# A two-layer transformer block with its follow-on block: weight splits reordered at the MLP entries, high halves first in narrow units

## The reference, cut to what matters

```python
h = x
for layer in range(2):
    hn = rms_norm(h, attn_norm[layer])
    ...                                        # attention
    h = h + merge_heads(mix) @ w_o[layer]
    h = h + squared_relu_mlp(rms_norm(h, mlp_norm[layer]), w_up[layer], w_down[layer])
x = rms_norm(h, final_norm)
mod = silu(c) @ w_ada + b_ada                  # 1024 x 9216
x = x + 0.5 * g1 * swiglu(modulate(rmsnorm(x), sh1, sc1), w_gate, w_up, w_down)
x = x + g2 * hybrid_mixer(modulate(rmsnorm(x), sh2, sc2), ...)
x = x + 0.5 * g3 * swiglu(modulate(rmsnorm(x), sh3, sc3), w_gate, w_up, w_down)
```

## Time and profile before

| what | value |
|---|---|
| median of 3 runs | 1197.65 us (1197.55, 1197.65, 1202.66) |
| the profiled execution: its own time | 1197.43 us |
| its span, first to last instruction | 1195.8 us |
| mean granted TensorE clock | 0.998 |
| DVE busy | 863.9 us (72%) |
| ACT busy | 652.5 us (55%) |
| POOL busy | 73.1 us (6%) |
| HBM traffic | 197 GB/s over the span |
| chain that ended last | PE 83%, DVE 8%, ACT 4%, issue 3%, DMA 1% |

### The profile page before, as it was taken

How to read it: one execution, slowest core, us unless ns; L and a number is a source line. 1 busy time by engine, 2 the same in 40 slices (tenths; PEclk the granted TensorE clock), 3 DMA queues, 4 the chain that set the end, 5 groups by cost and what they waited for, 6 DMA issues and landing times.

```text
span 1195.8 us, 17774 instructions
## 1 busy us (share of the span) xinstructions
PE 1165.1 (97%) x6763; PEld 1012.5 (85%) x6763; DVE 863.9 (72%) x1243; ACT 652.5 (55%) x883; POOL 73.1 (6%) x112
## 2 busy tenths in 40 slices
PE   8999999999999999999999999999999999999997
PEld 7898888888888888888888888888988888888886
DVE  6687799888767778988476765567986866655655
ACT  5556546555545555556565444547746755545453
POOL 9200011110000001110000000000000000000000
PEclk9999999999999999999999999999999999999999
DMA  7733699997463269997635565544661153655560
GB/s 253 229 109 124 228 333 351 316 316 251 150 192 130 71 214 352 338 320 252 212 106 190 198 207 179 195 146 145 195 209 39 32 197 122 211 179 195 168 216 36
DMA packets 143238, 236.33 MB, mean 198 GB/s; under 512 B 6357, under 2 KB 106950, under 8 KB 143174
## 3 DMA queue, kind: packets, MB, share of 16 engines
q1 hardware_dynamic: 130402, 196.73, 49.1%
q0 software_dynamic: 10400, 37.77, 8.7%
q10 hardware_dynamic: 2372, 0.96, 0.3%
HBM read 234.37 MB, written 1.05 MB: 197 GB/s over the span
## 4 chain that ended last, share of the span: by engine, by line
PE 83%; DVE 8%; ACT 4%; issue 3%; DMA 1%; POOL 0%; DVEq 0%; POOLq 0%; ACTq 0%
PE ps L2308 17%; PE ps L2062 9%; PE ps L2064 9%; PE ps L2066 9%; PE ps L2311 9%; DVE wlo L1120 3%; PE ps L1952 3%; PE ps L1954 3%; PE ps L1953 3%; PE ps L1999 2%; PE ps L2000 2%; PE ps L2001 2%; ACT whi L626 2%; PE ps L2151 1%; PE ps L2153 1%
## 5 line engine op out<-in xcount | busy, mean ns | idle before, releaser
L1120 DVE TENSOR_TENSOR wlo<-raw,whi 128x2048 fp32r<-128x2048 f32 (+2 forms) x185 | 414.9, 2258 | 134.4 <-ACT whi L626 133.9
L626 ACT ACTIVATE whi<-raw 128x2048 fp32r<-128x2048 f32 (+2 forms) x185 | 348.2, 1888 | 140.0 <-PE ps L2066 59.1
L2308 PE MATMUL ps<-a,whi 128*128 128x512 f32 x1024 | 255.7, 392 | 1.4 <-DVE wlo L1120 1.4
L2308 PEld LDWEIGHTS ps<-a,whi 128*128 128x128 f32 x1024 | 186.9, 189 | 37.0 <-issue 1.8
L2311 PEld LDWEIGHTS ps<-a,wlo 128*128 128x128 f32 x1024 | 139.8, 191 | 9.9
L2311 PE MATMUL ps<-a,wlo 128*128 128x256 f32 x1024 | 142.8, 283 | 0.0
L2062 PE MATMUL ps<-whi,hh 128*128 128x512 f32 x376 | 117.0, 393 | 3.5 <-DVE wlo L1120 3.5
L2064 PE MATMUL ps<-wlo,hh 128*128 128x512 f32 x376 | 116.3, 390 | 0.0
L2066 PE MATMUL ps<-whi,hl 128*128 128x512 f32 x376 | 116.1, 390 | 0.0
L1592 DVE SCALAR_TENSOR_TENSOR stage<-stage,cact 128x1024 f32<-128x1024 f32 x63 | 80.7, 1281 | 4.9 <-DMA stage<-in_w_ada_dram 3.6
L2064 PEld LDWEIGHTS ps<-wlo,hh 128*128 128x128 f32 x376 | 70.6, 188 | 15.2
(11 more groups left out here) (436 smaller groups left out, 1965.7 us busy)
## 6 DMA issues: line engine op xcount, KB each, us to landing
stage<-in_w_ada_dram POOLq DMA_DIRECT2D x72, 512.0 KB, 5.5
raw<-in_w_up_dram SPq DMA_DIRECT2D x32, 1024.0 KB, 6.7
raw<-in_w_down_dram SPq DMA_DIRECT2D x32, 1024.0 KB, 7.3
raw<-in_ffn_w_gate_dram SPq DMA_DIRECT2D x22, 1024.0 KB, 5.4
raw<-in_ffn_w_up_dram SPq DMA_DIRECT2D x22, 1024.0 KB, 5.4
raw<-in_ffn_w_down_dram SPq DMA_DIRECT2D x22, 1024.0 KB, 5.1
raw<-in_moba_w_qkv_dram SPq DMA_DIRECT2D x11, 1024.0 KB, 6.6
raw<-in_w_in_dram SPq DMA_DIRECT2D x10, 1024.0 KB, 5.2
```

What stands on the lines that cost most here:

```text
L626: A.activation(whi[:, s, 0:size], raw[:, s, 0:size], ACT.Copy).then_inc(w_hi, 1)
L1120: V.tensor_tensor(wlo[:, s, 0:size], raw[:, s, 0:size], whi[:, s, 0:size].bitcast(F32), ALU.subtract).then_inc(w_lo, 1)
L2308: T.matmul(bank(b + m), wh[:, c, m * P:(m + 1) * P], a2[:, c].rearrange("p k n -> p (k n)"), start=(c == 0), stop=False)
```

## The change

Six edits:

1. `a_unit` on PE: the loop is turned. For all eight tiles c and both column halves m it does the two matmuls with high weights first, waiting only for `w_hi`; then it waits for `w_lo` and does the 16 matmuls with low weights. In the very first unit this is done for c = 0 to 3 with `first_hi` and `first_lo`, then for c = 4 to 7.
2. `first_body` of both MLPs on DVE: the split of the first down unit n0+2 is done in two halves, the first with a semaphore of its own (`down_lo`); PE's first `d_unit` waits for that before k = 0 and for `w_lo` before k = 1.
3. `body(1)` of both MLPs on DVE is written out, and in it the addition (or fold) that stood between `hl` and the two splits stands between the two splits.
4. First chunk of both FFNs, on ACT and DVE: the split of unit n0+3 (the second up unit) moves ahead of the chunk; that of n0+4 stays behind it.
5. In the mixer on DVE the copy L1828 moves ahead of the split of unit U_Z+2.
6. The semaphore `down_lo` is added.

```diff
@@ -252,6 +252,7 @@
         in_ready = sem("in_ready")
         up_hi = sem("up_hi")
         up_lo = sem("up_lo")
+        down_lo = sem("down_lo")
         dstep = sem("dstep")
         astep = sem("astep")
         pstep = sem("pstep")
@@ -900,9 +901,11 @@
                         n_at = lambda q: n + q + 3 * FFN_BODY * i if isinstance(i, int) else (n + q, i)
                         split(n_at(0), slot(n))
                         if isinstance(i, int) and i == 0 and j == 0:
+                            split(n_at(1), slot(n + 1))
                             chunk(c0, n0 + 2, 4, True, 0)
-                        else:
-                            gated_chunk(i * FFN_BODY + (c0 + j), i * FFN_BODY + (k0 + j), i * (3 * FFN_BODY) + (n0 + 3 * j), j)
+                            split(n_at(2), slot(n + 2))
+                            continue
+                        gated_chunk(i * FFN_BODY + (c0 + j), i * FFN_BODY + (k0 + j), i * (3 * FFN_BODY) + (n0 + 3 * j), j)
                         for q in (1, 2):
                             split(n_at(q), slot(n + q))
                 body(0)
@@ -1502,8 +1505,13 @@
 
                 def first_body():
                     chunk(c0, 4, False, 0)
-                    for q in range(2):
-                        split(n0 + 2 + q, slot(n0 + 2 + q))
+                    s, half = slot(n0 + 2), UNIT // 2
+                    dve.wait_ge(w_hi, n0 + 3)
+                    V.tensor_tensor(wlo[:, s, 0:half], raw[:, s, 0:half], whi[:, s, 0:half].bitcast(F32),
+                                    ALU.subtract).then_inc(down_lo, 1)
+                    V.tensor_tensor(wlo[:, s, half:UNIT], raw[:, s, half:UNIT], whi[:, s, half:UNIT].bitcast(F32),
+                                    ALU.subtract).then_inc(w_lo, 1)
+                    split(n0 + 3, slot(n0 + 3))
                     k = 0
                     for j in range(1, MLP_BODY):
                         dve.wait_ge(p_copied_low, k0 + j)
@@ -1525,6 +1533,7 @@
 
                 def body(i, with_ada=True):
                     k = 0
+                    late = isinstance(i, int) and i == 1
                     for j in range(MLP_BODY):
                         cs = i * MLP_BODY + (c0 + j)
                         kw = i * MLP_BODY + (k0 + j)
@@ -1537,17 +1546,18 @@
                         dve.wait_ge(h_sq, cs + 1)
                         dve.wait_ge(h_hi, cs + 1)
                         V.tensor_tensor(flat(hl[:, j]), hs, flat(hh[:, j]).bitcast(F32), ALU.subtract).then_inc(h_ready, 1)
-                        if with_ada:
-                            if k < CT:
-                                ada_add(i + b0, k)
-                                k += 1
-                            else:
-                                ada_fold(i + b0)
                         for q in range(2):
+                            if with_ada and q == (1 if late else 0):
+                                if k < CT:
+                                    ada_add(i + b0, k)
+                                    k += 1
+                                else:
+                                    ada_fold(i + b0)
                             u = n0 + 2 * j + 2 + q
                             split(u + 2 * MLP_BODY * i if isinstance(i, int) else (u, i), slot(u))
                 first_body()
-                with dve.Fori(1, nb) as i:
+                body(1)
+                with dve.Fori(2, nb) as i:
                     body(i)
                 for i in range(nb, (CH1 - 1) // MLP_BODY):
                     body(i, False)
@@ -1563,9 +1573,11 @@
                         u_at = lambda q: u + q + 3 * FFN_BODY * i if isinstance(i, int) else (u + q, i)
                         split(u_at(0), slot(u))
                         if isinstance(i, int) and i == 0 and j == 0:
+                            split(u_at(1), slot(u + 1))
                             chunk(c0, 4, True, 0)
-                        else:
-                            gated_chunk(i * FFN_BODY + (c0 + j), i * FFN_BODY + (k0 + j), j)
+                            split(u_at(2), slot(u + 2))
+                            continue
+                        gated_chunk(i * FFN_BODY + (c0 + j), i * FFN_BODY + (k0 + j), j)
                         for q in (1, 2):
                             split(u_at(q), slot(u + q))
                 body(0)
@@ -1822,10 +1834,10 @@
             ins.then_inc(krope_done, 1)
 
             conv_taps(5)
-            splits(U_Z + 2)
             dve.wait_ge(xs_T, 1)
             dve.wait_ge(krope_done, 1)
             V.tensor_copy(xs[:, 1], banks(2, D)).then_inc(xs_tok2, 1)
+            splits(U_Z + 2)
             splits(U_Z + 3)
             dve.wait_ge(mqk_T, 1)
             for b in range(4):
@@ -1936,22 +1948,29 @@
 
 
 
-                if stage_name == "attn0":
-                    pe.wait_ge(first_lo, 1)
-                else:
-                    unit_wait(n)
                 wh, wl = w_view(whi, s, CT, AW), w_view(wlo, s, CT, AW)
-                for m in range(AW // P):
-                    o = ps[:, b, m * S:(m + 1) * S]
-                    for c in range(CT):
-                        if stage_name == "attn0" and m == 0 and c == 4:
-                            unit_wait(n)
-                        if stage_name and m == 0 and c % 2 == 0:
+                outs = [ps[:, b, m * S:(m + 1) * S] for m in range(AW // P)]
+                step = CT // 2 if stage_name == "attn0" else CT
+                for c0 in range(0, CT, step):
+                    if stage_name == "attn0" and c0 == 0:
+                        pe.wait_ge(first_hi, 1)
+                    else:
+                        pe.wait_ge(w_hi, n + 1)
+                    for c in range(c0, c0 + step):
+                        if stage_name and c % 2 == 0:
                             pe.wait_ge(in_ready, PAIR0[stage_name] + c // 2 + 1)
-                        wmh, wml = wh[:, c, m * P:(m + 1) * P], wl[:, c, m * P:(m + 1) * P]
-                        T.matmul(o, wmh, xh[:, c], start=(c == 0), stop=False)
-                        T.matmul(o, wmh, xl[:, c], start=False, stop=False)
-                        ins = T.matmul(o, wml, xh[:, c], start=False, stop=(c == CT - 1))
+                        for m, o in enumerate(outs):
+                            wmh = wh[:, c, m * P:(m + 1) * P]
+                            T.matmul(o, wmh, xh[:, c], start=(c == 0 and m == 0), stop=False)
+                            T.matmul(o, wmh, xl[:, c], start=False, stop=False)
+                    if stage_name == "attn0" and c0 == 0:
+                        pe.wait_ge(first_lo, 1)
+                    else:
+                        unit_wait(n)
+                    for c in range(c0, c0 + step):
+                        for m, o in enumerate(outs):
+                            ins = T.matmul(o, wl[:, c, m * P:(m + 1) * P], xh[:, c], start=False,
+                                           stop=(c == CT - 1 and m == AW // P - 1))
                 ins.then_inc(w_used, 1)
 
             def entry_unit(n, s, b, xh, xl, stage_name, tile=None, within=None):
@@ -2046,12 +2065,18 @@
                         elif u == 1:
                             ins.then_inc(half_done, 1)
 
-            def d_unit(n, s, b0, kn, width, xh, xl, c0, first, last, stage_name=None, per_t=2):
-
-                unit_wait(n)
+            def d_unit(n, s, b0, kn, width, xh, xl, c0, first, last, stage_name=None, per_t=2, halves=None):
+
+                if halves is None:
+                    unit_wait(n)
                 wh, wl = w_view(whi, s, kn, width), w_view(wlo, s, kn, width)
                 for k in range(kn):
                     c = c0 + k
+                    if halves is not None:
+                        if k == 0:
+                            pe.wait_ge(down_lo, halves)
+                        else:
+                            unit_wait(n)
                     if stage_name and c % 2 == 0:
                         pe.wait_ge(in_ready, PAIR0[stage_name] + c // 2 + 1)
                     for t in range(TT):
@@ -2340,7 +2365,8 @@
                             return
                         pe.wait_ge(h_ready, i * MLP_BODY + (c0 + j + 1))
                         d_unit(u + 1 if st_ else (u + 1, i), slot(u + 1), 0, 2, D, hh[:, j], hl[:, j], 0,
-                               st_ and i == 0 and j == 0, False)
+                               st_ and i == 0 and j == 0, False,
+                               halves=(1 if n0 == U_MLP0 else 2) if st_ and i == 0 and j == 0 else None)
 
                 entry_unit(n0, slot(n0), 4, ah, al, stage_name, within=lambda: late_T(1 if n0 == U_MLP0 else 3))
                 body(0)
```

## The result

The changed kernel takes **1189.64 us** in the median (four executions, 1189.54 to 1189.76). The kernel before, run beside it on the same chip, has a median of 1197.6 us (four executions, 1197.06 to 1202.66). The ratio is 0.9917, 95% interval 0.9899 to 0.9935: a gain of 0.83% (0.65% to 1.01%). The quotient of the two medians is 0.9934, a gain of 0.66%; the kernel before varies by several us from execution to execution, and four of them fix its median poorly. The direction was right, every edit can be found in the trace, and the gain was taken too small.

The account below looks back on a forecast made before the run. PE, busy 97% of the span, was taken as the bound. Its removable waits, 1.54 + 0.63 + 2.90 + 1.42 + 0.82 - 0.1 = 7.2 us, from 1197.43 gave 1190.2, median 1190.4, range 1189.3 to 1193.7.

Parts of the forecast that it names:

- The start: First narrow units: PE begins near 10.05 us with high weights, 2.5 us won, of which 1.54 us stay.
- The wait for the diagonal: Row-norm matmul after the first narrow units: its diagonal is ready at 22.59, so PE newly waits about 1 us.
- The first down unit in halves: MLP entries: the first half is ready 1.1 us sooner, so waits of 0.35 and 0.28 go, 0.63 us.
- tight spot: Second body of each MLP: the split PE needs just fits, 0.0 to 0.1 us margin; 0.1 us deducted for both.
- a down unit near 175 still waits: Second body of the first MLP: the sign that the reordered addition fails to remove PE's wait, forecast gain 2.90 us.
- FFN: Entries of both FFNs: the second up unit is split early, all of PE's 0.71 us wait at each goes, 1.42 us.
- mixer: Key transposes of the mixer: the copy ends before PE is done with its unit, so the 0.82 us wait goes.
- only idle time of PE can be won: Whole kernel: PE is busy 97% of the span, so only its idle time, some 31 us, can be won.
- lies 0.22 us under the median, so the median comes to 1190.4: Whole kernel: step from the profiled execution's 1197.43 us, forecast 1190.2, to a forecast median of 1190.4.
- Edit 3's 2.90 us: Second bodies of both MLPs: the addition moved between the splits removes PE waits of 1.55 and 1.35 us.
- the wait inside the MLP: Rival at the second bodies: the reordering brings nothing, as ACT's high part or a tile is late; 1193.3 us, chance 0.17.
- low matmuls in a row: Rival in narrow units: 16 consecutive low matmuls expose weight loads, 0.07 us each, 20 us in all; 1210.8 us, chance 0.04.

Follow-up runs that it names:

- e7b: The changed kernel with one more stop of PE, for its own last matmul, in each of the 18 narrow units; 1195.11 us, ratio 0.9964.
- e8b: The changed kernel with two added stops of PE for its own last matmul in each narrow unit, 36 in all; 1199.56 us, ratio 0.9978.
- e16: The changed kernel with DVE's split that PE awaits in both second MLP bodies delayed by one and a half units of subtraction; 1200.99 us, ratio 1.0013.
- e1: The kernel before with only the narrow units changed to take all high weights first; 1197.41 us, ratio 0.9979.
- e2: The kernel before with only the first down unit's split done in two halves (DVE and PE); 1201.45 us, ratio 1.0029.
- e4: The kernel before with only the second up unit of each FFN split ahead of the first chunk; 1196.78 us, ratio 0.9965.
- e5b: The kernel before with only the mixer's copy of the x branch moved ahead of a split; 1199.04 us, ratio 1.0012.
- e13b: The changed kernel without the reordering of the second MLP body on DVE; 1195.65 us, ratio 0.9950.
- e14: The changed kernel with DVE's split that PE awaits in both second MLP bodies delayed by half a unit of subtraction; 1192.46 us, ratio 0.9941.
- e15: The changed kernel with DVE's split that PE awaits in both second MLP bodies delayed by a whole unit of subtraction; 1197.49 us, ratio 0.9977.

## Where the prediction was right, and the two steps that failed

- **The start**: 1.54 forecast, 1.32 measured. The wait for the diagonal came as predicted; the diagonal is ready at 22.63, not 22.59, and PE starts 0.15 us behind it, where the prediction took 0.05. The mechanism held and the term was 0.22 us too large; what makes the 0.15 us, and the 0.08 lost up to the first head, no run shows.
- **The first down unit in halves**: 0.63 forecast as a gain of its own; worth 0.1 at most beside edit 3. The prediction saw that PE would come earlier at the second body, by 0.35 us, and called it a tight spot: 0.1 us for both. It left 0.20 and 0.25 us of idle time, and so its own sign against edit 3, "a down unit near 175 still waits", came in part. In the first MLP the difference is the hidden 0.25 us of the stop that went at the entry: PE came 0.60 us earlier and the split was ahead of need by 0.4. The halves cost what was said, 139.78 + 1.22 - 138.65 = 2.35 us against 2.29. An estimate by the formula of the Trainium skill (VectorE: DVE Perf Modes, "The TRN2 errata"), 2 x (1024 + 151) / 0.96 ns, is 2.45 us; the measurement decides for the row.
- **Edits 2 and 3 together**: 3.43 forecast with the tight spots, 1.92 + 1.63 = 3.55 in this pair of executions. The idle time that went is 0.35 + 1.35 + 0.28 + 1.10 = 3.08, as 0.20 and 0.25 us stay at the second bodies; the two stops that went wholly (142 and 447 us) bring another 0.25 us each. That the sum came out within 0.12 us is luck: the tight spots took 0.35 us more than forecast, and the hidden part of the stops gave 0.5 us back.
- **FFN**: 1.42 forecast, 0.96 + 0.95; **mixer**: 0.82, measured 1.02. Idle time of 0.71, 0.71 and 0.82 was all won, and 0.20 to 0.25 us with each.
- So the first step that failed is "only idle time of PE can be won": outside the start every term of the sum is the idle time in a bracket and nothing more. Five stops gone, at 0.25 us (the rate of e7b and e8b), are the 1.2 us between 6.5 and 5.3.
- The second, and the larger one for the ratio, is the sentence that the profiled execution "lies 0.22 us under the median, so the median comes to 1190.4". Edit 3's 2.90 us are right only for an execution with stops of 1.55 and 1.35 us. Their length comes from transfers, and in 49 of 86 executions the mean clock is the one that goes with one or two falls (0.995 to 0.997): 2 us more in the median of the next group, 4 in the one after. (Eleven more lie lower still, see below.) The median of all 86 is 1200.0 us, 2.3 us above the one that was taken as the base; 1189.64 of 1200.0 is 0.991, as the measured ratio says. The three executions that the prediction had (1197.55, 1197.65, 1202.66) showed that spread already, and it was not asked what it was.
- The rivals: the wait inside the MLP shrank but did not all go, as the split waits for ACT's high part (0.57 us at 474.55) or, in other executions, for the second tile; low matmuls in a row run at 0.120 us.

**Open.** The 11 executions at 0.989 and under, 9.5 us above the first group: no profile caught one, and e16, whose clock falls twice, never went under 0.993. From 0.998 to 0.988 is some 24 us at the lower level (an estimate: 0.010 of 1206 us, at half the clock), so it takes more than two falls of 3.4 us. The kernels of the experiments that lack the second body's order (e1, e2, e4, e5b, e13b) had five such in 45 executions, those that have it none in 64, which points to the same place but doesn't show it.

## What to carry to other kernels

A wait that went back to a DMA had no fixed length here (1.04 to 2.62 us over twelve stops): take such a wait from several executions, and read the mean clock of each beside its time. Where PE's order leaves it waiting behind such a transfer, put the work that PE needs ahead of it; the gain is then the wait, what the clock loses behind a long one, and the spread. In this kernel some 0.25 us went with each stop of PE that went, on top of the idle time that the rows show, and a new stop costs the same. A wait that only grows longer or shorter has no such extra (e14: stops 2.71 us longer, span 2.7 longer). And when a stop goes, ask whether PE comes to the next wait earlier and stands there instead.

## What the runs showed of the hardware that was not expected

- The granted clock fell to one half for some 3.4 us behind single PE stops of 2.52, 2.59, 2.61, 2.62, 3.79 and 3.85 us in an otherwise busy kernel, and stayed full behind one of 2.54 and behind those of 2.09 us and less. One fall costs some 1.6 us. That the length of the stop decides is shown for this place of the kernel by e14, e15 and e16.
- It does not begin with the first matmul behind the stop: in e2 it begins at 176.6, 0.5 us before PE's first matmul at 177.08; in e16 the first rows behind 177.61 are of full speed and the clock falls at 178.8. It lasted 3.4 us in either case.
- A stop of PE for its own last result costs 0.31 us, of which 0.06 is idle time by the trace; one of 0.20 us made by DVE costs 0.45.
